# Attention of two mixers: probabilities turned by products with a diagonal of reciprocal sums, values in two parts with swapped banks

## The reference, cut to what matters

```
s = einsum(q, k) * ATTN_SCALE            # 256 queries x keys, masked
m = s.max(-1); p = exp(s - m); den = p.sum(-1)
num = einsum(p, v);  o = num / den
# mixer A: three groups (windows 128, 512, 2048; dilations 1, 4, 16), joined by
#   wgt = den * exp(m - m.max over groups), normalised: one softmax over all three
# mixer B: causal over the 256 tokens (one block)
return o @ w_o
```

## Time and profile before

| | |
|---|---|
| median of 3 runs | 1086.56 us (1086.34 to 1087.43) |
| the profiled execution | 1087.44 us, span 1085.4 us |
| PE busy | 1075.8 us, 99% |
| PE weight loads | 909.5 us, 84% |
| DVE busy | 800.9 us, 74% |
| ACT busy | 669.1 us, 62% |
| POOL busy | 112.2 us, 10% |
| DMA, mean | 169 GB/s |

### The profile page before, as it was taken

How to read it: one execution, slowest core, us unless ns; L and a number is a source line. 1 busy time by engine, 2 the same in 40 slices (tenths; PEclk the granted TensorE clock), 3 DMA queues, 4 the chain that set the end, 5 groups by cost and what they waited for, 6 DMA issues and landing times.

```text
span 1085.4 us, 18425 instructions
## 1 busy us (share of the span) xinstructions
PE 1075.8 (99%) x6484; PEld 909.5 (84%) x6484; DVE 800.9 (74%) x1390; ACT 669.1 (62%) x1185; POOL 112.2 (10%) x127
## 2 busy tenths in 40 slices
PE   9999999999999999999999999999999999999998
PEld 8967899998988887888888888888877788888887
DVE  5977765555567767666765989888876758998886
ACT  5477654445565657566566666666766656666664
POOL 0000000000000000000010323222001012232220
PEclk9999999999999999999999999999999999999999
DMA  9642566656646563365524466665563435666562
GB/s 309 198 136 79 175 183 203 181 188 180 193 125 210 165 194 117 99 196 185 171 70 154 156 196 192 195 193 178 172 194 103 151 115 166 186 212 193 175 195 95
DMA packets 117773, 183.87 MB, mean 169 GB/s; under 512 B 6864, under 2 KB 70736, under 8 KB 117584
## 3 DMA queue, kind: packets, MB, share of 16 engines
q1 hardware_dynamic: 117280, 182.77, 53.8%
q10 hardware_dynamic: 432, 0.29, 0.1%
HBM read 181.99 MB, written 1.05 MB: 169 GB/s over the span
## 4 chain that ended last, share of the span: by engine, by line
PE 89%; DVE 6%; ACT 2%; DMA 1%; issue 1%; SPq 0%; DVEq 0%; ACTq 0%
PE ps L754 11%; PE ps L725 11%; PE ps L727 10%; PE ps L726 10%; PE ps L759 9%; PE ps L818 5%; PE ps L820 5%; PE ps L819 5%; PE ps L757 4%; PE ps L758 4%; DVE hid L2482 2%; DVE w_lo L1951 2%; PE ps L920 2%; PE ps L897 1%; PE ps L950 1%; PE ps L993 1%
## 5 line engine op out<-in xcount | busy, mean ns | idle before, releaser
L1951 DVE TENSOR_TENSOR w_lo<-w_stage,w_hi 128x1024 fp32r<-128x1024 f32 x336 | 415.0, 1252 | 146.9 <-ACT w_hi L1306 146.2
L1306 ACT ACTIVATE w_hi<-w_stage 128x1024 fp32r<-128x1024 f32 x336 | 350.7, 1055 | 141.6 <-PE ps L727 75.1
L759 PE MATMUL ps<-aT,w_lo 128*128 128x256 f32 x992 | 279.1, 281 | 0.0
L754 PE MATMUL ps<-aT,w_hi 128*128 128x512 f32 x640 | 227.2, 399 | 1.1 <-DVE w_lo L1951 1.1
L725 PE MATMUL ps<-w_hi,aT 128*128 128x512 f32 x480 | 192.9, 402 | 2.1 <-DVE aT L1965 1.6
L759 PEld LDWEIGHTS ps<-aT,w_lo 128*128 128x128 f32 x992 | 188.3, 190 | 0.6
L727 PE MATMUL ps<-w_hi,aT 128*128 128x512 f32 x480 | 187.5, 391 | 0.0
L726 PE MATMUL ps<-w_lo,aT 128*128 128x512 f32 x480 | 187.0, 390 | 0.0
L754 PEld LDWEIGHTS ps<-aT,w_hi 128*128 128x128 f32 x640 | 120.2, 188 | 31.8 <-issue 3.0
L1919 POOL TENSOR_TENSOR o_sb<-xn,o_sb 128x256 f32<-128x256 f32 x80 | 90.8, 1156 | 274.6 <-DVE xn L2360 212.5
L725 PEld LDWEIGHTS ps<-w_hi,aT 128*128 128x128 f32 x480 | 90.1, 188 | 25.7 <-issue 6.3
(11 more groups left out here) (257 smaller groups left out, 1349.3 us busy)
## 6 DMA issues: line engine op xcount, KB each, us to landing
w_stage<-in_ffn_w_up SPq DMA_DIRECT2D x88, 512.0 KB, 4.6
w_stage<-in_a_w_qkv SPq DMA_DIRECT2D x72, 512.0 KB, 4.0
w_stage<-in_ffn_w_down SPq DMA_DIRECT2D x44, 512.0 KB, 3.6
w_stage<-in_w_up SPq DMA_DIRECT2D x32, 512.0 KB, 3.8
w_stage<-in_w_down SPq DMA_DIRECT2D x32, 512.0 KB, 4.2
w_stage<-in_b_w_qkv SPq DMA_DIRECT2D x24, 512.0 KB, 3.8
w_stage<-in_w_in SPq DMA_DIRECT2D x23, 512.0 KB, 4.8
w_stage<-in_w_out SPq DMA_DIRECT2D x8, 512.0 KB, 3.6
```

Source lines behind the costliest of these rows:

```text
L754: pe.matmul(ps[:, bank(stg, names[f]), :], wh, aT[:, k, :, :].rearrange("p a s -> p (a s)"), start=(k == 0), stop=False)
L759: last = pe.matmul(o, wl, aT_hi[:, k, :], start=False, stop=(k == KT - 1))
L1306: act.activation(w_hi[:, slot, :], w_in[:, slot, :], ACT.Copy).then_inc(hi_done[slot], 1)
L1951: dve.tensor_tensor(w_lo[:, slot, :], w_in[:, slot, :], w_hi[:, slot, :].bitcast(F32), ALU.subtract).then_inc(lo_done[slot], 1)
```

## The change

**Turning.** The transposition against the identity becomes a matrix product with a diagonal that holds the reciprocal sums, so a probability is turned and normalised at once. The diagonals are 64x64: DVE multiplies `ident_pair` (two 64-wide identities on top of each other, made once by POOL) with the reciprocals, two (A) or four (B) per unit (`scales`). Each 128x128 tile is turned as four 64x64 tiles; query rows 0 to 63 go to bank 4 and 64 to 127 to bank 5.

**Values.** Products have 64 rows and 64 columns. Key rows 0 to 63 and 64 to 127 are summed in two parts: in part 0 row half r writes bank X or Y by r, in part 1 the banks are swapped, so each bank gets both halves in turn. Part 1 waits for part 0 by the semaphore `crossed`. The banks X and Y (6 and 7) hold query half 0 and 1 and are both used by every pair of heads. In step u PE's order is scores(u+1), values part 0, turn(u-1), values part 1, and then `behind`; the values of pair j stand in step u = per * (j + 2).

**Outputs.** ACT rounds each bank to `oT_hi`, DVE subtracts to `oT_lo`, two of 128x128 per pair of heads. `turned_ring` is four deep. Gone: POOL's spreading and subtraction, the turning of the sums, the output product and its copies.

**Order on DVE and ACT.** DVE: maxima(u+1), copy of pB(u-1), `scales`(u), the weight split at u = n-1, outputs. ACT: copy of pA(u-1), the weight split at u = n-1, output copies, exps(u+1).

```
@@ PE @@
+            def turn_unit(stg, un, v):
+                banks = [bank(stg, f"p{r}{v}") for r in "AB"]
+                for r in "AB":
+                    pe.wait_ge(*is_free(stg, f"p{r}{v}"))
+                pe.wait_ge(s["diag"], at(stg, "diag", v + 1))
                 for h in range(2):
                     for t in range(3):
-                        last = pe.transpose(ps[:, b, t * P:(t + 1) * P],
-                                            score_ring[v % 3][:, h, t * P:(t + 1) * P], ident)
+                        d0 = (2 * un["scaled"][t] + h) * HP
+                        for r in range(2):
+                            rows_ = slice(r * HP, (r + 1) * HP)
+                            for c in range(2):
+                                c0 = t * P + c * HP
+                                last = pe.matmul(ps[c * HP:(c + 1) * HP, banks[r], (3 * h + t) * HP:(3 * h + t + 1) * HP],
+                                                 score_ring[v % 3][rows_, h, c0:c0 + HP],
+                                                 diag[rows_, v % 3, d0:d0 + HP], start=True, stop=True)
...
+            def values(stg, units, j, part):
+                banks = [bank(stg, f"o{z}{j}") for z in "XY"]
+                if part == 1:
+                    pe.wait_ge(s["crossed"], at(stg, "crossed", j + 1))
+                if part == 0:
+                    for z in "XY":
+                        pe.wait_ge(*is_free(stg, f"o{z}{j}"))
+                    for r in "AB":
+                        pe.wait_ge(*is_drained(stg, f"p{r}{units[0]['per'] * (j + 1) - 1}"))
+                items = {(r, h): value_items(units, j, r ^ part, r, h) for r in range(2) for h in range(2)}
+                n = len(items[0, 0])
+                for m in range(n):
+                    for r in range(2):
+                        for h in range(2):
+                            w, src, cols_ = items[r, h][m]
+                            last = pe.matmul(ps[h * HD:(h + 1) * HD, banks[r ^ part], cols_], w, src,
+                                             start=(part == 0 and m == 0), stop=(part == 1 and m == n - 1))
...
             def attention(stg, units, v_names, behind):
+                n, per = len(units), units[0]["per"]
+                for u in range(1, n + per + 1):
                     if u + 1 < n:
                         scores(stg, units[u + 1], u + 1)
+                    j = values_at(u, units)
+                    if j is not None:
...
+                        values(stg, units, j, 0)
+                    if u <= n:
+                        turn_unit(stg, units[u - 1], u - 1)
+                    if j is not None:
+                        values(stg, units, j, 1)
                     if u in behind:
                         behind[u]()
@@ ACT @@
                     if u == n - 1:
                         split(stg, last)
+                    j = values_at(u, units)
+                    if j is not None:
+                        for z in range(2):
+                            un, name = units[per * j], f"o{'XY'[z]}{j}"
+                            act.wait_ge(*is_full(stg, name))
+                            act.activation(heads_to(oT_hi, un, z), heads_from(bank(stg, name), un), ACT.Copy)\
+                                .then_inc(s["ohi"], 1)
                     if u + 1 < n:
                         exps(stg, units[u + 1], u + 1)
@@ DVE @@
+            def scales(stg, un, v):
+                m = 2 * len(un["queries"])
+                rden = stat(f"rden{v % 3}", 4)[:, 0:m]
+                dve.wait_ge(s["prob"], at(stg, "prob", 2 * v + 2))
+                dve.reciprocal(rden, stat(f"den{v % 2}", 4)[:, 0:m]).then_inc(s["rd"], 1)
+                dve.wait_ge(s["rd"], at(stg, "rd", v + 1))
+                dve.tensor_tensor(diag[:, v % 3, 0:m * HP].rearrange("p (m c) -> p m c", c=HP),
+                                  ident_pair[:].unsqueeze(1).broadcast_to([P, m, HP]),
+                                  rden.unsqueeze(2).broadcast_to([P, m, HP]), ALU.mult).then_inc(s["diag"], 1)
...
             def attention(stg, units, last):
+                scales(stg, units[0], 0)
+                for u in range(1, n + per + 1):
+                    if u + 1 < n:
+                        maxima(stg, units[u + 1], u + 1)
                     if u <= n:
...
+                        dve.tensor_copy(turned_ring[v % 4][:, 1, :], ps[:, b, 0:3 * P]).then_inc(drained[b], 1)
+                    if u < n:
+                        scales(stg, units[u], u)
                     if u == n - 1:
                         split(stg, last)
+                    j = values_at(u, units)
+                    if j is not None:
+                        for z in range(2):
...
+                            dve.wait_ge(s["ohi"], at(stg, "ohi", 2 * j + z + 1))
+                            dve.tensor_tensor(heads_to(oT_lo, un, z), heads_from(b, un),
+                                              heads_to(oT_hi, un, z).bitcast(F32), ALU.subtract).then_inc(drained[b], 1)
```

More of the change, by code:

```diff
@@ L451, in blocks_kernel @@
             "orstd", "osq", "hms", "dm", "ovar", "sig", "sq", "ms8", "rs8", "silu", "u", "uhi", "ulo", "msq", "pms", "prstd", "x_new",
-            "half", "scaled", "r2", "lam", "zeroed", "const_ready", "gate_w", "unit", "rd", "rdb", "bc", "ohi", "olo")}
+            "half", "scaled", "r2", "lam", "zeroed", "const_ready", "gate_w", "unit", "rd", "diag", "pair", "crossed", "ohi")}
         def is_full(stg, name, i=0):
@@ L932, in own_values @@
-            def own_values(un, v, b):
-                turned, qt = turned_ring[v % 2], un["queries"][0]
-                for half in range(2):
-                    q = half * HP
-                    for h in range(2):
-                        c = un["at"] + h * HD
-                        last = pe.matmul(ps[h * HD:(h + 1) * HD, b, qt * P + q:qt * P + q + HP],
-                                         v_own(qt, half)[:, c:c + HD], turned[:, h, S + q:S + q + HP],
-                                         start=False, stop=(half == 1))
-                return last
@@ L944, in unit_values @@
-            def unit_values(un, v, b):
-                turned = turned_ring[v % 2]
-                q0, n = un["queries"][0] * P, len(un["values"])
-                for m, (t, c, at_, W) in enumerate(un["values"]):
-                    for h in range(2):
-                        last = pe.matmul(ps[h * HD:(h + 1) * HD, b, q0 + at_:q0 + at_ + W],
-                                         vv[:, t, c + h * HD:c + (h + 1) * HD],
-                                         turned[:, h, un["turned"][m]:un["turned"][m] + W],
-                                         start=(m == 0), stop=(m == n - 1 and not un["own"]))
-                return own_values(un, v, b) if un["own"] else last
+                        d0 = (2 * un["scaled"][t] + h) * HP
@@ new lines, in turn_unit @@
+                        for r in range(2):
[5 more added lines that the diff above has]
+                                                 diag[rows_, v % 3, d0:d0 + HP], start=True, stop=True)
+                            if (h, t) == (1, 2):
+                                last.then_inc(full[banks[r]], 1)
@@ new lines, in values @@
+            def values(stg, units, j, part):
[15 more added lines that the diff above has]
+                                             start=(part == 0 and m == 0), stop=(part == 1 and m == n - 1))
+                        if part == 1 and m == n - 1:
+                            last.then_inc(full[banks[r ^ part]], 1)
+                if part == 0:
+                    last.then_inc(s["crossed"], 1)
@@ L1388, in attention @@
                 n, per = len(units), units[0]["per"]
-                for u in range(1, n + 4):
+                for u in range(1, n + per + 1):
                     if u <= n:
@@ L2043, in attention @@
             def attention(stg, units, last):
                 n, per = len(units), units[0]["per"]
-                for u in range(1, n + 3):
+                dve.wait_ge(s["pair"], 1)
+                scales(stg, units[0], 0)
+                for u in range(1, n + per + 1):
+                    if u + 1 < n:
+                        maxima(stg, units[u + 1], u + 1)
                     if u <= n:
                         v = u - 1
-                        m = 2 * len(units[v]["queries"])
                         b = bank(stg, f"pB{v}")
-                        dve.wait_ge(s["prob"], at(stg, "prob", 2 * v + 2))
-                        dve.reciprocal(stat(f"rden{v % 3}", 4)[:, 0:m], stat(f"den{v % 2}", 4)[:, 0:m])\
-                            .then_inc(s["rd"], 1)
-                        if u + 1 < n:
-                            maxima(stg, units[u + 1], u + 1)
@@ L2060, in attention @@
-                    if i == 0 and 0 <= j < n // per:
-                        b = bank(stg, f"o{j}")
-                        dve.wait_ge(s["bc"], at(stg, "bc", j + 1))
-                        if j >= 2:
```

(5 more changed lines are left out.)

125 lines of the change are left out of this document (44 added, 81 removed).

## The result

The changed kernel takes **1101.18 us** (median of 4 runs, 1100.55 to 1102.66) where the kernel before took 1086.84 beside it: ratio 1.0136 [1.0124, 1.0148], 14.3 us slower.

The account below looks back on a forecast made before the run. PE's queue was taken to bound the kernel; new waits cancel its 9.5 us saving, leaving 2 x 0.0 (mixer A halves) + 2 x 1.8 (mixer B halves) = +3.6 us, so 1090.2 us; range 1085 to 1096.

Parts of the forecast that it names:

- What bounds the kernel: Whole kernel: PE, busy 99% of the span, bounds it; a change counts by what it does to PE's queue.
- The change, PE's work: Attention: turns 0.70 us, values unchanged at 0.67, shape switches within attention gone; 9.5 us gained if PE alone decided.
- L908's 16 passes in 0.41: Scores row, before the change: taken as showing a round of four 64-wide passes costs 0.058 us.
- the walk: Attention halves step by step: A 24.5 against 24.5 us, B +1.8 each, +3.6 in all; chance 0.78 for +1 to +7.
- The new wait: Before every turn, PE waits for DVE's copy, reciprocal and diagonal: 1.23 us in mixer A, 1.36 in B, partly covered.
- One output bank pair: Mixer B: values of j = 2 wait for DVE's subtractions behind its weight split, a stall of 1.6 us a half.
- Rival B: Attention: PE's work alone decides, -9.5 us, 1077; chance 0.13 for it or a good part of it.
- the loop: From one turn's end to the next's start, through DVE's copy, reciprocal and diagonal: 1.23 us in mixer A, 1.36 in B.
- The check by load: Mixer A, per pair of units: DVE has 4.1 us of steps, PE 4.05 of work, ACT 3.8.
- Rival C: Turns and values: the small products don't go four abreast, +19 us, 1106; chance 0.09.

Follow-up runs that it names:

- e8_half_wide: Changed kernel with each turn made of 12 products of 64x64 tiles by 128 columns instead of 24 by 64, half the blocks not turned: 1092.46 us.
- e3_split_late: Changed kernel with ACT and DVE splitting the coming weight behind that step's output copies and subtractions, not ahead of them: 1098.17 us.
- e11: Changed kernel, diagonal made before DVE's copy, split behind outputs, turns of 12 double-wide products against constant identities, no wait for the diagonal: 1089.55 us.
- e5_turn12: Changed kernel with each pair of 64x64 turn products made as one product of 64 rows by 128 columns: 1110.33 us.

## Why the prediction was wrong

**What bounds the kernel: right**, and so was the direction (0.65 for slower). The range missed by 5 us.

**The change, PE's work: the array time was right, the price incomplete.** Turns 0.70 forecast, 0.71 measured; values 0.67 and 0.67; no changes of shape; a half of A 20.95 against 21.3. The step that failed is the sentence "24 products of 64x64x64, six rounds of two passes: 12 x 0.058": it costs products by the columns they move and lets their number be free. The 0.70 itself held wherever no stop fell in a turn; what failed is that the supply of instructions stood in the sum at nothing. L908's 16 passes in 0.41 only showed that a short burst runs at that rate. The earlier trace rows held the count, 6484 passes; the change makes 7908 of them, all the new ones in some 90 us. The term of the sum that was left out measures 7.7 us by e8_half_wide and 8.1 by adding the stops, against a whole miss of 14.3 - 3.6 = 10.7. Of the other 3.0, mixer A's waits and its work make about 2.5: without late blocks a half of A would have been some 1.25 above before (25.73 + 8 x 0.04 against 24.80), where the walk had 0.0.

**The new wait: right in mechanism, 0.17 us short.** 1.23 us forecast, 1.40 measured: copy to reciprocal 0.47, reciprocal to diagonal 0.19 and diagonal 0.29 as forecast; PE to the waiting copy 0.30 in place of 0.21 (the value), and the wake-up of PE 0.15 in place of the estimated 0.06. In the first half of A of e8_half_wide the six waits before turns are 0.73, 0.74, 0.74, 0.62, 0.74 and 0.44 us from product to product, together 4.0 against 3.3 forecast (0.59, 0.57, 0.57, 0.40, 0.56, 0.61). With 0.33 more before the first part of the values of j = 2, where a block of instructions begins, that is about the 0.9 us by which this half exceeds the kernel before, where I had found nothing left of the gain and nothing lost.

**One output bank pair: right in mechanism.** 1.6 forecast; 1.70 measured from product to product, of which 0.33 stands at every change from dense products to values, so 1.37, behind DVE's split and subtractions. e3_split_late removed it and gave 1.36 in the half without a stop. A half of B was to lose 1.8 and loses 1.74 in e8_half_wide, in part by luck: its first turn waits 1.05 where 0.73 stood, and that makes up for the 1.37. Without most of the late instructions the halves lose 5.3 us, and e8_half_wide's 1092.46, or 1093.4 with the 1.0 of array time that it saves, lies inside the range of 1085 to 1096.

**Rival B (PE's work alone)** could not come about: with the instructions of a turn halved and the loop out of the way e11 stands at 1089.55. The check by load in the prediction said why, DVE 4.1 us of steps a pair against PE's 4.05; it should have weighed more against B. **Rival C is false**: four tiles go abreast with column neighbours on the same rows, 48 passes in 0.71. The Trainium skill (TensorE: Matmul & The Clock Gate, Part 3, The mechanism) would have a load overlap a running product only across row groups. Here neighbours that share their rows overlap, and e5_turn12, whose neighbours alternate between row groups, is four times slower per pass.

## What to carry to other kernels

Count the instructions of an engine per microsecond beside its busy time: when work is cut into smaller tiles, the block supply is a resource of its own, and here PE could not be fed more than 256 instructions in 3.3 to 4.3 us. Its mark in a profile is idle time put down to "issue" in the middle of a group with no semaphore, at intervals of 256 instructions, and two stretches of the same code with different idle times; where the block ends just at a wait, it bears the semaphore's name. And before pricing a gain on the engine that bounds, add up the load of the next one in the same stretch: DVE was at 4.1 us a pair before PE fell to 4.05, so at most a part of PE's saved work was ever to be had.

## What the runs showed of the hardware

- A block of 256 PE instructions comes as one 16 KB packet, 2.3 to 2.7 us before PE goes on from a stop of the changed kernel, and at best every 3.3 us. Between stops that follow each other the packet starts 1.2 to 1.6 us after PE has gone on from the last one (431.95 to 433.32, 435.95 to 437.52, 440.23 to 441.79, 563.84 to 565.05), so here the next block was not under way while PE stood still. What sets these times, and whether a block can be asked for earlier, stays open. Which products are hit depends on where the 256th instruction falls: two halves with the same products differ by 2.64 us.
- Float32 passes of 64 columns: 0.015 us each in four 64x64 tiles, 0.062 each in tiles of 64 rows by 128 columns, though these also alternate between two row halves.
- Rounds of 128 columns in 64x64 tiles cost 0.67 / 6 = 0.11, so a product twice as wide costs the same array time per column with half the instructions.
